# A ring of ten weight places split into six for gate/up and four for down, the down chunks issued by the scalar engine

## The chip, the cores and the metric
One core of a Trainium2 chip. The metric is the time of one execution on the device in microseconds; the median of three runs stands for a kernel.

## The reference
One decoder layer in fp32 for 288 tokens: 256 prompt tokens and 32 sample tokens (8 requests of 4) that read a paged cache. Three sub-layers, each followed by `LayerNorm(alpha * x + sublayer(x))`:

```python
mix  = merge_groups(moba(qa, ka, va), stick_breaking(qb, kb, vb), g_moba, g_sb, w_out)  # 16 heads of 64
x    = layer_norm(alpha * x + mix, ln1_g, ln1_b)
x    = layer_norm(alpha * x + mem_attend(x, mk, mv, w_mq, w_mo), ln2_g, ln2_b)           # 4 heads of 256, 256 memory tokens
...
logits = h @ w_router + b_router                      # 32 experts, the best 4 of each token
gate, up = split(h @ w_gu[e] + b_gu[e], 2)            # w_gu[e]: 1024 x 2048
act  = (clip(up, -7, 7) + 1) * min(gate, 7) * sigmoid(1.702 * min(gate, 7))
y    = act @ w_down[e] + b_down[e]                    # w_down[e]: 1024 x 1024
x    = layer_norm(alpha * x + sum of the 4 experts' y, weighted by their gates, ln3_g, ln3_b)
```

The weights of all 32 experts are read once: 8 MB of `w_gu` and 4 MB of `w_down` each, 403 million bytes in all.

## The kernel before
The program is written engine by engine with semaphores. Its first part (projections, both kinds of attention, the cross-attention) streams its inputs through six slots of 1 MB (`EARLY`, in the order of the list `ITEMS`) on the sync queue (SP). GpSimd (POOL) issues smaller loads and the stores of keys and values. Its first loads bring the rows of the norms' vectors into `vec_rows`, which TensorE turns into the columns of `vec` (wait on `vec_in` in line 662). Four of these loads (line 1288) bring the second norm's two vectors once more, every second element of each, for the pairs of columns that the gathered rows of the experts use (`by_seat`, line 2290).

The second part is the expert stage. An expert's weights come as six chunks of 2 MB: four of gate/up (256 rows of `w_gu` each) and two of down (512 rows of `w_down` each). There are ten places (`ALL`, `PLACES`, `chunk_slot`), and chunk `i`, counted over the experts in the order in which they run, takes place `i % 10`; so the place of a chunk was last held by the chunk ten before it. The sync engine issues all of them in this order (lines 1247 to 1259). Ahead of each it waits until the place is free (`slot_free`): `chunk_used` counts what TensorE has finished with, `gu_used` and `dn_used` stand for an expert's last gate/up and last down chunk, raised by VectorE and ScalarE. The first ten chunks are loaded while the first part ends, by `first_chunk`.

An expert runs in passes over at most 64 rows ("wide") or 32 ("narrow", two of four experts after the first group; `KINDS`), as many as its tokens need. All passes of an expert use the same chunks, and a place counts as free only in the last pass (`passes_done` in `enter`). The first four experts run in their own order, wide; the other 28 are sorted by the number of their tokens into an order of alternating wide and narrow ones (`order`, computed on the chip).

In a pass TensorE multiplies three gate/up chunks (line 1080), adds the output of the pass before (`combine`, lines 1014 and 1017), multiplies the fourth chunk, gathers the rows of the next pass (lines 1025 and 1033), turns the activations (1115) and multiplies the two down chunks (1125 in wide passes, 1129 in narrow ones). VectorE and ScalarE compute the activation in between; ScalarE's pass begins with the sigmoid (line 1815) and ends with the copy of the result out of bank 4, behind which it raises `dn_used`.

Of the kernel before, what the change touches and what calls it, by code (L numbers as in the profile page):

```python
# [68 lines left out]
HOME = 9760  # L69
PLACES = (8, 9, 6, 3, 0, 5, 7, 4, 1, 2)  # L70
EARLY = 6
# [84 lines left out]
def build(nc, A, O):  # L156
    ctx = ExitStack()
    with ctx:
        def sb(name, shape, dt=F32):
            return ctx.enter_context(nc.sbuf_tensor(name, shape, dt))  # L160

        def sem(name):
            return ctx.enter_context(nc.semaphore(name))
# [4 lines left out]
        pages = sb("pages", [1, NB_DEC * PAGES], I32)  # L168
        vec = sb("vec", [P, 56])
        small = sb("small", [P, 32])  # L170
# [17 lines left out]

        def chunk_slot(i):

            at = HOME + PLACES[i % ALL] * SLOT
# [33 lines left out]
        tmp = [at_place(6, 768 * i, 768) for i in range(5)] + [at_place(7, 768 * i, 768) for i in range(3)]  # L225
        vec_rows = at_place(6, 3840, P)[0:56]
        so = [at_place(7, 2304 + 512 * g, 512) for g in range(2)]
# [70 lines left out]
        gpick = [table("rot", P), table("new_strict", P), carve(mem, 6912, P)]  # L298
        ln3 = carve(mem, HOME + PLACES[NE * CHUNKS_E % ALL] * SLOT, 2, D)


        const_in = sem("const_in")
        pages_in = sem("pages_in")
        vec_in = sem("vec_in")
        early_in = [sem(f"early_in{i}") for i in range(EARLY)]
        item_used = sem("item_used")
        slot_in = [sem(f"slot_in{i}") for i in range(ALL)]
# [4 lines left out]
        dn_used = sem("dn_used")  # L312
        bank_full = [sem(f"bank_full{i}") for i in range(ROT)]
# [192 lines left out]
        def gu_src(e, k):  # L506
            return A["w_gu"][0, bass.ds(e, 1), 256 * k:256 * k + 256, :].rearrange("a (p r) n -> p (a r n)", p=P)
# [8 lines left out]
        def _(pe):  # L516
# [144 lines left out]
            pe.sem_inc(item_used, 4)  # L661
            pe.wait_ge(vec_in, 16 * 10)
            last, full = turn_blocks(("vec",), [vec_rows[:, :]])
# [379 lines left out]

            pe.sem_inc(chunk_used, CHUNKS_E - 2)
            pe.wait_ge(z_ready, 3)
# [11 lines left out]
            def chunk_arrived(group, q, j):  # L1057

                i = CHUNKS_E * (group * GROUP + q) + j
                pe.wait_ge(slot_in[i % ALL], 16 * (i // ALL + 1))  # L1060
                return chunk_slot(i)

# [6 lines left out]
            def expert_pass(group, q, kind):  # L1069
# [50 lines left out]
                for i in range(DN_CHUNKS):  # L1120
                    w = chunk_arrived(group, q, GU_CHUNKS + i).rearrange("p (r n) -> p r n", r=4)
                    for r in range(4):
                        for h in range(2):
                            if kind == CAP:
                                last = pe.matmul(bank[4][64 * h:64 * h + 64, :], actT[:, r, 64 * i:64 * i + 64],  # L1125
                                                 w[:, r, 512 * h:512 * h + 512], start=(i + r == 0), stop=(i == 1 and r == 3))
                            else:
                                at, t = 64 * h + 32 * (r % 2), 2 * i + r // 2
                                last = pe.matmul(bank[4][at:at + 32, :], actT[:, r % 2, 32 * t:32 * t + 32],  # L1129
                                                 w[:, r, 512 * h:512 * h + 512], start=(i == 0 and r < 2), stop=(i == 1 and r >= 2))  # L1130
                    if i == 0:
                        last.then_inc(chunk_used, 1)
                        turn_seats(n + 1)
# [23 lines left out]
        def _(sp):  # L1157
# [27 lines left out]

            def chunk(e, i):

                j = i % CHUNKS_E
                src = gu_src(e, j) if j < GU_CHUNKS else dn_src(e, j - GU_CHUNKS)
                sp.dma_start(chunk_slot(i), src).then_inc(slot_in[i % ALL], 16)  # L1190

            def first_chunk(i):
                chunk(i // CHUNKS_E, i)

# [39 lines left out]
            def slot_free(j, n):  # L1234

                if j == GU_CHUNKS - 1:
                    sp.wait_ge(gu_used, n)
                elif j == CHUNKS_E - 1:
                    sp.wait_ge(dn_used, n)
                else:  # L1240
                    sp.wait_ge(chunk_used, n * (CHUNKS_E - 2) + (j + 1 if j < GU_CHUNKS else j))

# [3 lines left out]

            for i in range(ALL, NE * CHUNKS_E + 1):
                if i == GROUP * CHUNKS_E:
                    sp.wait_ge(order_ready, 1)
                if i % CHUNKS_E == 0 or i == ALL:  # L1250
                    e = i // CHUNKS_E
                    if GROUP <= e < NE:
                        e = sp.value_load(order[0:1, e:e + 1], min_val=0, max_val=NE - 1)
                before, j = divmod(i - ALL, CHUNKS_E)
                if j == 0:
                    enter(before)
                slot_free(j, sp.snap(passes_done))
                if i < NE * CHUNKS_E:
                    chunk(e, i)
            for i, name in enumerate(("ln3_g", "ln3_b")):  # L1260
# [12 lines left out]
        def _(pool):  # L1273
# [211 lines left out]
        def _(act):  # L1485
# [122 lines left out]
            last.then_inc(read_sem(("vs",)), 1)  # L1608
            carry(("vec",), vec[:, :], wide(56))
            act.wait_ge(keys_stored, 16 * 2)  # L1610
# [200 lines left out]
            def expert_pass(kind):  # L1811
                n = act.snap(blocks_done)
                width = D * kind // P
                act.wait_ge(sig_in, n + 1)
                act.activation(sig_s[:, 0:width], gate_s[:, 0:width], ACT.Sigmoid, scale=SW_ALPHA).then_inc(sig_ready, 1)  # L1815
                act.wait_ge(sel_turned, n + 2)
                copy(selT, bank[5][:, 0:NPT])
                for h in range(2):
                    last = copy(sel_end[64 * h:64 * h + 64, h, :], bank[5][64 * h:64 * h + 64, NPT:T])
                last.then_inc(selT_ready, 1)  # L1820
                act.wait_ge(act_turned, n + 1)
                copy(actT[:, 0:width // P, :], bank[3][:, 0:width].rearrange("p (a b) -> p a b", b=P)).then_inc(actT_ready, 1)
                seats_in(n + 1)
                act.wait_ge(down_done, n + 1)
                act.sem_inc(dn_used, 1)
                copy(y_s, bank[4][:, :]).then_inc(y_ready, 1)
                act.reg_add(blocks_done, blocks_done, 1)

            def expert(e, kind):
                passes = act.value_load(passes_at[0:1, bass.ds(e, 1)], min_val=1, max_val=-(-T // kind))  # L1830
                with act.Fori(0, passes):
                    expert_pass(kind)

            for e in range(GROUP):
# [29 lines left out]
        def _(dve):  # L1864
# [424 lines left out]

            def by_seat(at):  # L2290
                return vec[:, at:at + KB].rearrange("p (h b) -> p b h", h=2).unsqueeze(3).broadcast_to([P, 4, 2, CAP])

            def seats_scale(n):

                dve.wait_ge(seats_turned, n + 1)
                x = xgT.rearrange("p (b h) s -> p b h s", h=2)
                dve.tensor_tensor(x, bank[0][:, :].rearrange("p (b h s) -> p b h s", b=4, h=2), by_seat(40), ALU.mult).then_inc(seats_scaled, 1)  # L2297
                dve.wait_ge(seats_scaled, n + 1)
                dve.tensor_tensor(x, x, by_seat(48), ALU.add).then_inc(xg_ready, 1)

# [178 lines left out]
```

## Time and profile before

| | |
|---|---|
| median of 3 runs | 1415.88 us (1411.34 to 1418.51) |
| the profiled execution | 1420.54 us, its span 1418.8 us |
| TensorE busy | 1303.4 us, 92% of the span |
| VectorE, ScalarE, GpSimd busy | 425.6, 238.1, 240.6 us |
| mean granted TensorE clock | 0.973 of full speed |
| read from HBM | 475.84 MB |
| copies, mean over the span | 340 GB/s |

The span runs from the first to the last instruction. A busy TensorE is not one at its peak. The DMA share is the mean busy share of the core's 16 copy engines in a stretch; it can read a little over 1. "SPq", "POOL" and "ACTq" with DMA_DIRECT2D are the instructions that issue a copy. An arrow in brackets names what ended the idle time before an instruction.

### The profile page before, as it was taken

Reading aid. Unit: us, or ns where it says so; the run is one execution under the profiler, and the core shown is the slowest. Engines: PE = TensorE matmul, PEld = TensorE weight load, DVE = VectorE, ACT = ScalarE, POOL = GpSimd, SP = SyncE. Lnnn points to the kernel's source line nnn. Section 1 sums busy time; section 2 is a strip of 40 time slices with the busy share of each in tenths; the row PEclk is TensorE's granted clock in tenths of the full one; section 3 lists DMA queues with packets and bytes.
Section 4 is the critical chain, followed back from the end, with each engine's and each line's share of the span. In section 5 each row is a group of like instructions: output and inputs, shape, how many; then the busy total and the mean of one; then the engine's idle time right before and its main releaser. Section 6 shows DMA issues by size and latency. Waiting matters only on the chain.

```text
span 1418.8 us, 22637 instructions
## 1 busy us (share of the span) xinstructions
PE 1303.4 (92%) x8246; PEld 637.7 (45%) x8246; DVE 425.6 (30%) x859; ACT 238.1 (17%) x537; POOL 240.6 (17%) x477
## 2 busy tenths in 40 slices
PE   6999688999889799999999999987999988899993
PEld 5787565677646333333333333322333333333331
DVE  1124544324432533223232132321131321222316
ACT  1124534211320201111110110100011100010102
POOL 4010001000101221212221122221121221122302
PEclk9999899999999799999999999999999999999997
DMA  9434429634489399999999999999999999999993
GB/s 253 142 123 151 150 84 333 204 119 148 181 327 418 143 399 428 431 430 430 428 430 432 431 429 431 430 429 431 430 423 429 431 431 428 431 432 415 429 430 137
DMA packets 73543, 482.74 MB, mean 340 GB/s; under 512 B 5146, under 2 KB 38098, under 8 KB 48658
## 3 DMA queue, kind: packets, MB, share of 16 engines
q1 hardware_dynamic: 71346, 475.29, 82.0%
q0 software_dynamic: 2064, 6.10, 1.3%
q8 instruction: 64, 1.05, 0.3%
q10 hardware_dynamic: 48, 0.13, 0.0%
q14 instruction: 21, 0.17, 0.0%
HBM read 475.84 MB, written 5.64 MB: 339 GB/s over the span
## 4 chain that ended last, share of the span: by engine, by line
PE 74%; DMA 18%; DVE 3%; issue 2%; ACT 2%; POOL 0%; SPq 0%; ACTq 0%; DVEq 0%; POOLq 0%; PEldq 0%
PE bank L1080 23%; DMA mem<-in_w_gu 13%; PE bank L547 10%; PE bank L1125 9%; PE bank L556 4%; PE bank L1025 4%; PE bank L1014 4%; DMA mem<-in_w_down 3%; PE bank L534 2%; PE bank L968 2%; PE bank L1129 2%; PE bank L1033 2%; DMA mem<-in_w_in 1%; PE bank L1115 1%; PE bank L1017 1%
## 5 line engine op out<-in xcount | busy, mean ns | idle before, releaser
L1080 PE MATMUL bank<-mem 128*32 128x256 f32 (+1 forms) x3136 | 419.6, 485 | 29.9 <-DMA mem<-in_w_gu 29.0
L1080 PEld LDWEIGHTS bank<-mem 128*32 128x32 f32 (+1 forms) x3136 | 152.2, 122 | 269.8 <-issue 200.2
L2360 DVE TENSOR_TENSOR mem<-mem,bank 128x512 f32<-128x512 f32 (+1 forms) x180 | 101.2, 627 | 431.9 <-PE bank L1014 431.9
L1497 ACT ACTIVATE mem<-bank 128x512 f32<-128x512 f32 (+7 forms) x236 | 114.2, 497 | 543.7 <-PE bank L1125 152.2
L547 PE MATMUL bank<-mem 128*128 128x288 f32 (+1 forms) x640 | 158.6, 405 | 7.1 <-PE bank L547 3.3
L1125 PE MATMUL bank<-mem 128*64 128x512 f32 x672 | 153.5, 598 | 0.0
L547 PEld LDWEIGHTS bank<-mem 128*128 128x128 f32 x640 | 121.4, 192 | 42.1 <-issue 8.4
L1438 POOL COPY mem<-mem 96x64 bf16 x35 | 11.5, 329 | 600.4 <-PE bank L1107 600.2
L1815 ACT ACTIVATE mem<-mem 128x512 f32<-128x512 f32 (+1 forms) x35 | 19.0, 544 | 491.3 <-DVE mem L2373 491.3
L2297 DVE TENSOR_TENSOR mem<-bank,vec 128x512 f32<-128x512 f32 x36 | 24.9, 691 | 201.8 <-PE bank L1041 201.8
L1878 DVE COPY mem<-bank 128x512 f32<-128x512 f32 (+3 forms) x82 | 47.5, 586 | 123.0 <-PE bank L534 37.7
L1125 PEld LDWEIGHTS bank<-mem 128*64 128x64 f32 x672 | 44.5, 136 | 84.0 <-issue 84.0
L534 PE MATMUL bank<-consts,mem 128*128 128x128 f32 (+3 forms) x449 | 58.7, 281 | 21.9 <-DMA mem<-in_x_prompt 7.3
L1025 PE MATMUL bank<-mem 128*64 128x512 f32 x288 | 74.4, 636 | 1.5 <-DVE mem L2263 1.5
L1014 PE MATMUL bank<-mem,consts 64*128 64x512 f32 x288 | 72.7, 623 | 1.0 <-ACT mem L1497 1.0
L556 PE MATMUL bank<-mem 128*128 128x256 f32 x256 | 62.5, 405 | 5.5 <-ACT mem L1497 5.5
L534 PEld LDWEIGHTS bank<-consts,mem 128*128 128x128 f32 (+3 forms) x449 | 50.1, 143 | 35.6 <-issue 29.3
L1434 POOL TENSOR_SCALAR mem<-mem 64x64 f32<-64x64 f32 (+1 forms) x140 | 64.7, 481 | 7.5 <-POOL mem L1428 7.5
L1447 POOL TENSOR_SCALAR consts<-mem 128x128 f32<-128x128 f32 x70 | 62.6, 899 | 7.5 <-POOL mem L1442 7.5
L556 PEld LDWEIGHTS bank<-mem 128*128 128x128 f32 x256 | 51.5, 204 | 15.7 <-issue 8.1
L1129 PE MATMUL bank<-mem 128*32 128x512 f32 x448 | 53.9, 598 | 1.7 <-DMA mem<-in_w_down 1.4
L1014 PEld LDWEIGHTS bank<-mem,consts 64*128 64x128 f32 x288 | 25.4, 190 | 43.2 <-issue 43.2
(246 smaller groups left out, 975.5 us busy)
## 6 DMA issues: line engine op xcount, KB each, us to landing
mem<-in_w_gu SPq DMA_DIRECT2D x128, 2048.0 KB, 25.5
mem<-in_w_down SPq DMA_DIRECT2D x64, 2048.0 KB, 26.6
mem<-in_w_in SPq DMA_DIRECT2D x12, 1024.0 KB, 9.9
mem<-in_w_mkv SPq DMA_DIRECT2D x8, 1024.0 KB, 9.3
mem<-in_cache_k SPq DMA_DIRECT2D x16, 512.0 KB, 7.2
mem<-in_cache_v SPq DMA_DIRECT2D x16, 512.0 KB, 5.8
mem<-in_cache_mem_k SPq DMA_DIRECT2D x8, 1024.0 KB, 4.8
mem<-in_cache_mem_v SPq DMA_DIRECT2D x8, 1024.0 KB, 5.6
```

The costliest lines, as they stand in the source:

```text
L534: last = pe.transpose(ps[0:cols, at:at + rows], src, C("ident", 0, rows, rows))
L547: last = pe.matmul(ps[:, 0:n], w[:, k, col:col + P], (mem_block(k) if src is None else src[:, k, 0:n]), start=(k == 0), stop=(k == KB - 1))
L556: last = pe.matmul(ps[0:r, 0:256], (mem_block(k) if src is None else src[:, k])[:, a:a + r], w[:, k, :], start=(k == 0), stop=(k == KB - 1))
L1014: pe.matmul(bank[COMB_BANK[2 * c + h]][:, :], selT[rows, P * c:P * c + P], y_s[rows, :], start=True, stop=True).then_inc(comb, 1)
L1025: pe.matmul(bank[0][64 * h:64 * h + 64, :], pick[:, c, :], z[:, c, :].rearrange("p (q h) -> p h q", h=2)[:, h], start=(c == 0), stop=False)
L1080: last = pe.matmul(to, ebias[0:96, 0:kind] if k is None else xgT[:, k, 0:kind], columns(src, j, t, kind), **flags)
L1125: last = pe.matmul(bank[4][64 * h:64 * h + 64, :], actT[:, r, 64 * i:64 * i + 64], w[:, r, 512 * h:512 * h + 512], start=(i + r == 0), sto ...
L1129: last = pe.matmul(bank[4][at:at + 32, :], actT[:, r % 2, 32 * t:32 * t + 32], w[:, r, 512 * h:512 * h + 512], start=(i == 0 and r < 2), s ...
L1434: pool.tensor_scalar(pick[0:r, c, :], slots_now[0:r, 0:CAP], rcol[0:r, c:c + 1], None, ALU.is_equal).then_inc(pool_step, 1)
L1447: pool.tensor_scalar(gpick[c], slots_now, rcol[:, c:c + 1], gcol[:, c:c + 1], ALU.is_equal, ALU.mult).then_inc(pool_step, 1)
L1497: return act.activation(out, in_, ACT.Copy, scale=scale)
L2360: dve.tensor_tensor(a, a, ps, ALU.add).then_inc(added, 1)
```

## The change
The ring of ten places is split: six for gate/up chunks (`GU_PLACES`) and four for down chunks (`DN_PLACES`), each with its own semaphores. The first ten loads are now the first expert's six, two gate/up chunks and both down chunks of the second. After that the sync engine issues gate/up chunks alone, each when the gate/up chunk six before it has been used. The down chunks of expert `e + 2` are issued by ScalarE (`next_down`) behind its last pass of expert `e`. `dn_used` is gone, and `chunk_used` counts three chunks a pass.

The four strided loads of the second norm's rows at the start are gone. In their place GpSimd issues two loads into a tile of its own, `pair_vec`, ahead of the loads of `b_gu`; VectorE waits for them once before the first expert.

```diff
-PLACES = (8, 9, 6, 3, 0, 5, 7, 4, 1, 2)
+GU_PLACES = (8, 9, 6, 3, 7, 4)
+DN_PLACES = (0, 5, 1, 2)
+GU_RING, DN_RING = len(GU_PLACES), len(DN_PLACES)
...
-        vec = sb("vec", [P, 56])
+        vec = sb("vec", [P, 40])
+        pair_vec = sb("pair_vec", [P, 2, 4, 2])
...
-            pe.wait_ge(vec_in, 16 * 10)
+            pe.wait_ge(vec_in, 16 * 6)
...
                     if i == 0:
-                        last.then_inc(chunk_used, 1)
                         turn_seats(n + 1)
...
             def first_chunk(i):
-                chunk(i // CHUNKS_E, i)
+                if i < 4:
+                    gate_up(0, i)
+                elif i in (6, 7):
+                    gate_up(1, i - 2)
+                else:
+                    d = {4: 0, 5: 1, 8: 2, 9: 3}[i]
+                    down(d // DN_CHUNKS, d)
...
                 if j == GU_CHUNKS - 1:
                     sp.wait_ge(gu_used, n)
-                elif j == CHUNKS_E - 1:
-                    sp.wait_ge(dn_used, n)
                 else:
-                    sp.wait_ge(chunk_used, n * (CHUNKS_E - 2) + (j + 1 if j < GU_CHUNKS else j))
+                    sp.wait_ge(chunk_used, n * (GU_CHUNKS - 1) + j + 1)
...
-            for i in range(ALL, NE * CHUNKS_E + 1):
+            for g in range(GU_RING, NE * GU_CHUNKS + 1):
...
-                before, j = divmod(i - ALL, CHUNKS_E)
+                before, j = divmod(g - GU_RING, GU_CHUNKS)
...
-            for name, at in (("ln2_g", 40), ("ln2_b", 48)):
-                for h in range(2):
-                    pool.dma_start(vec_rows[at + 4 * h:at + 4 * h + 4, :], A[name][0].rearrange("(a p h) -> h a p", p=P, h=2)[h],
-                                   allow_slow_non_contiguous=True).then_inc(vec_in, 16)
...
             await_fill(pool, ("o", PAIR_ORDER[-2]))
+            for i, name in enumerate(("ln2_g", "ln2_b")):
+                pool.dma_start(pair_vec[:, i], A[name][0].rearrange("(b p h) -> p b h", p=P, h=2), allow_slow_non_contiguous=True).then_inc(pair_vec_in, 16)
             for part in range(3):
                 pool.dma_start(bgu_f[32 * part:32 * part + 32, :], A["b_gu"][0]).then_inc(bias_in, 16)
...
                 act.wait_ge(down_done, n + 1)
-                act.sem_inc(dn_used, 1)
                 copy(y_s, bank[4][:, :]).then_inc(y_ready, 1)
...
+            def next_down(e, i):
+
+                for d in range(DN_CHUNKS):
+                    at = DN_CHUNKS * i + d
+                    act.dma_start(dn_place(at), dn_src(e, d)).then_inc(dn_in[at % DN_RING], 16)
...
             for e in range(GROUP):
                 expert(e, FIRST[e])
+                if e + 2 < GROUP:
+                    next_down(e + 2, e % 2)
+                else:
+                    if e + 2 == GROUP:
+                        act.wait_ge(order_ready, 1)
+                    next_down(act.value_load(order[0:1, e + 2:e + 3], min_val=0, max_val=NE - 1), e % 2)
-            act.wait_ge(order_ready, 1)
-            with act.Fori(GROUP // 2, NE // 2) as pair:
+            with act.Fori(GROUP // 2, NE // 2 - 1) as pair:
                 for i in range(2):
                     expert(pair * 2 + i, KINDS[i])
+                    next_down(expert_at(pair * 2 + i + 2), i)
+            for i in range(2):
+                expert(NE - 2 + i, KINDS[i])
...
+            dve.wait_ge(pair_vec_in, 16 * 2)
```

## Rows read from the trace of the kernel before

**Rows 1.** The page: one engine's total, and GB/s in 40 slices.
```profile
PE 1303.4 (92%) x8246; PEld 637.7 (45%) x8246; DVE 425.6 (30%) x859; ACT 238.1 (17%) x537; POOL 240.6 (17%) x477
...
GB/s 253 142 123 151 150 84 333 204 119 148 181 327 418 143 399 428 431 430 430 428 430 432 431 429 431 430 429 431 430 423 429 431 431 428 431 432 415 429 430 137
```

**Rows 2.** Stretches: from:to, length, engines' busy time (count), clock, DMA share, GB/s.
```profile
510.00:520.00 10.00, 10.00 (x54) 3.76 (x54) 1.38 (x2) 1.79 (x3) 4.23 (x9) 1.00 0.92 360
...
494.00:1392.00 898.00, 867.91 (x5893) 320.06 (x5889) 233.18 (x393) 100.98 (x244) 186.96 (x374) 0.99 1.00 427
200.00:240.00 40.00, 32.62 (x272) 21.42 (x273) 15.07 (x34) 14.64 (x28) 3.68 (x9) 0.91 0.72 248
```

**Rows 3.** Timeline of TensorE: start, length, what; a wide, a narrow, a double expert.
```profile
605.39 7.04 PE L1080 MATMUL bank<-mem 128*64 128x512 f32 x32
...
634.28 3.83 PE L1080 MATMUL bank<-mem 128*32 128x256 f32 x64
...
642.48 2.02 PE L1080 MATMUL bank<-mem 128*32 128x256 f32 x32
...
652.70 2.79 PE L1080 MATMUL bank<-mem 128*64 128x512 f32 x12
...
750.25 8.78 PE L1080 MATMUL bank<-mem 128*64 128x512 f32 x32 [2.76 <-DMA mem<-in_w_gu]
...
765.93 3.65 PE L1080 MATMUL bank<-mem 128*64 128x512 f32 x16
...
781.39 7.04 PE L1080 MATMUL bank<-mem 128*64 128x512 f32 x32
```

**Rows 4.** The page's groups of instructions: the down products of wide passes.
```profile
L1125 PE MATMUL bank<-mem 128*64 128x512 f32 x672 | 153.5, 598 | 0.0
```

**Rows 5.** Waits: who, for whom: us in total, times, longest.
```profile
PE bank L882 <- DMA mem<-in_cache_mem_v: 2.9, 1, 2.9
...
ACT mem L1815 <- DVE mem L2373: 491.3, 35, 21.4
```

**Rows 6.** Stretches of the start, columns as in rows 2.
```profile
9.00:21.00 12.00, 10.63 (x50) 8.15 (x48) 1.41 (x4) 1.76 (x4) 7.31 (x5) 1.00 1.19 129
25.00:40.00 15.00, 14.70 (x54) 11.04 (x55) 2.75 (x6) 1.06 (x3) 0.00 (x0) 0.90 1.09 384
```

**Rows 7.** Timeline of TensorE at the start.
```profile
24.73 5.72 PE L547 MATMUL bank<-mem 128*128 128x288 f32 x16 [2.90 <-DMA mem<-in_w_in]
...
30.77 4.04 PE L547 MATMUL bank<-mem 128*128 128x288 f32 x16
```

**Rows 8.** Timeline of the sync queue and of ScalarE in the expert stage.
```profile
493.89 0.33 SPq L1190 DMA_DIRECT2D mem<-in_w_down  x1
...
515.07 0.33 SPq L1190 DMA_DIRECT2D mem<-in_w_gu  x1
...
519.35 0.60 ACT L1497 ACTIVATE mem<-bank 128x512 f32<-128x512 f32 x1 [7.26 <-PE bank L1125]
...
785.18 0.33 SPq L1190 DMA_DIRECT2D mem<-in_w_down  x1
...
810.57 0.33 SPq L1190 DMA_DIRECT2D mem<-in_w_gu  x1
```

**Rows 9.** One line's copies, from 485 to 560 us: issue to landing.
```profile
DMA to landing us min/median/max: 7.7/11.2/14.3
```

**Rows 10.** DMA issues: queue, count, KB each, median us to landing.
```profile
mem<-in_w_mo SPq DMA_DIRECT2D x4, 1024.0 KB, 14.0
...
out_new_k_prompt<-mem POOLq DMA_DIRECT2D x1, 1024.0 KB, 4.6
...
out_mem_v_prompt<-mem POOLq DMA_DIRECT2D x1, 1024.0 KB, 7.7
out_mem_k_prompt<-mem POOLq DMA_DIRECT2D x1, 1024.0 KB, 9.3
```

**Rows 11.** Timeline of TensorE: the last down products.
```profile
1393.32 1.92 PE L1129 MATMUL bank<-mem 128*32 128x512 f32 x16 [0.57 <-DMA mem<-in_w_down]
```

More of the change, by code:

```diff
@@ L187, in carve, with gu_place, dn_place @@
             return v
-        def chunk_slot(i):
-            at = HOME + PLACES[i % ALL] * SLOT
+        def gu_place(g):
+            at = HOME + GU_PLACES[g % GU_RING] * SLOT
+            return mem[:, at:at + SLOT]
+        def dn_place(d):
+            at = HOME + DN_PLACES[d % DN_RING] * SLOT
             return mem[:, at:at + SLOT]
@@ L225, in build @@
         tmp = [at_place(6, 768 * i, 768) for i in range(5)] + [at_place(7, 768 * i, 768) for i in range(3)]
-        vec_rows = at_place(6, 3840, P)[0:56]
+        vec_rows = at_place(6, 3840, P)[0:40]
         so = [at_place(7, 2304 + 512 * g, 512) for g in range(2)]
@@ L298, in build @@
         gpick = [table("rot", P), table("new_strict", P), carve(mem, 6912, P)]
-        ln3 = carve(mem, HOME + PLACES[NE * CHUNKS_E % ALL] * SLOT, 2, D)
+        ln3 = gu_place(NE * GU_CHUNKS)[:, 0:2 * D].rearrange("p (a n) -> p a n", a=2)
         const_in = sem("const_in")
@@ L304, in build @@
         vec_in = sem("vec_in")
+        pair_vec_in = sem("pair_vec_in")
         early_in = [sem(f"early_in{i}") for i in range(EARLY)]
         item_used = sem("item_used")
-        slot_in = [sem(f"slot_in{i}") for i in range(ALL)]
+        gu_in = [sem(f"gu_in{i}") for i in range(GU_RING)]
+        dn_in = [sem(f"dn_in{i}") for i in range(DN_RING)]
         bias_split = sem("bias_split")
@@ L311, in build @@
         gu_used = sem("gu_used")
-        dn_used = sem("dn_used")
         bank_full = [sem(f"bank_full{i}") for i in range(ROT)]
@@ L1042, in turn_seats @@
                 last.then_inc(seats_turned, 1)
-            pe.sem_inc(chunk_used, CHUNKS_E - 2)
+            pe.sem_inc(chunk_used, GU_CHUNKS - 1)
             pe.wait_ge(z_ready, 3)
@@ L1057, in chunk_arrived @@
             def chunk_arrived(group, q, j):
-                i = CHUNKS_E * (group * GROUP + q) + j
-                pe.wait_ge(slot_in[i % ALL], 16 * (i // ALL + 1))
-                return chunk_slot(i)
+                e = group * GROUP + q
+                if j < GU_CHUNKS:
+                    g = GU_CHUNKS * e + j
+                    pe.wait_ge(gu_in[g % GU_RING], 16 * (g // GU_RING + 1))
+                    return gu_place(g)
+                d = DN_CHUNKS * e + j - GU_CHUNKS
+                pe.wait_ge(dn_in[d % DN_RING], 16 * (d // DN_RING + 1))
+                return dn_place(d)
             def columns(v, j, t, kind):
@@ L1184, in early, with gate_up, down @@
                     sp.dma_start(dst, src[0, item[1]].rearrange("(c p) h d -> p c (h d)", p=P)).then_inc(s, 16)
[L1186 to L1190, printed above, removed]
+            def gate_up(e, g):
+                sp.dma_start(gu_place(g), gu_src(e, g % GU_CHUNKS)).then_inc(gu_in[g % GU_RING], 16)
+            def down(e, d):
+                sp.dma_start(dn_place(d), dn_src(e, d % DN_CHUNKS)).then_inc(dn_in[d % DN_RING], 16)
             def first_chunk(i):
-                chunk(i // CHUNKS_E, i)
+                if i < 4:
[5 more added lines that the diff above has]
+                    down(d // DN_CHUNKS, d)
             for i, item in enumerate(ITEMS):
@@ L1237, in slot_free @@
                     sp.wait_ge(gu_used, n)
-                elif j == CHUNKS_E - 1:
-                    sp.wait_ge(dn_used, n)
                 else:
-                    sp.wait_ge(chunk_used, n * (CHUNKS_E - 2) + (j + 1 if j < GU_CHUNKS else j))
+                    sp.wait_ge(chunk_used, n * (GU_CHUNKS - 1) + j + 1)
             def enter(at):
                 sp.reg_add(passes_done, passes_done, sp.value_load(passes_at[0:1, at:at + 1], min_val=1, max_val=PASS_MAX))
-            for i in range(ALL, NE * CHUNKS_E + 1):
-                if i == GROUP * CHUNKS_E:
+            for g in range(GU_RING, NE * GU_CHUNKS + 1):
+                if g == GROUP * GU_CHUNKS:
                     sp.wait_ge(order_ready, 1)
-                if i % CHUNKS_E == 0 or i == ALL:
-                    e = i // CHUNKS_E
+                if g % GU_CHUNKS == 0 or g == GU_RING:
+                    e = g // GU_CHUNKS
                     if GROUP <= e < NE:
                         e = sp.value_load(order[0:1, e:e + 1], min_val=0, max_val=NE - 1)
-                before, j = divmod(i - ALL, CHUNKS_E)
+                before, j = divmod(g - GU_RING, GU_CHUNKS)
                 if j == 0:
@@ L1257, in _ @@
                 slot_free(j, sp.snap(passes_done))
-                if i < NE * CHUNKS_E:
-                    chunk(e, i)
+                if g < NE * GU_CHUNKS:
+                    gate_up(e, g)
             for i, name in enumerate(("ln3_g", "ln3_b")):
@@ L1608, in _ @@
             last.then_inc(read_sem(("vs",)), 1)
-            carry(("vec",), vec[:, :], wide(56))
+            carry(("vec",), vec[:, :], wide(40))
             act.wait_ge(keys_stored, 16 * 2)
@@ L1832, in expert, with expert_at @@
                     expert_pass(kind)
+            def next_down(e, i):
+                for d in range(DN_CHUNKS):
+                    at = DN_CHUNKS * i + d
+                    act.dma_start(dn_place(at), dn_src(e, d)).then_inc(dn_in[at % DN_RING], 16)
+            def expert_at(at):
+                return act.value_load(order[0:1, bass.ds(at, 1)], min_val=0, max_val=NE - 1)
             for e in range(GROUP):
                 expert(e, FIRST[e])
-            act.wait_ge(order_ready, 1)
-            with act.Fori(GROUP // 2, NE // 2) as pair:
+                if e + 2 < GROUP:
[5 more added lines that the diff above has]
+            with act.Fori(GROUP // 2, NE // 2 - 1) as pair:
                 for i in range(2):
                     expert(pair * 2 + i, KINDS[i])
+                    next_down(expert_at(pair * 2 + i + 2), i)
+            for i in range(2):
+                expert(NE - 2 + i, KINDS[i])
             load_table(ACT.Sqrt)
@@ L2288, in _, with by_seat @@
             dve.tensor_tensor(gates, expo, small[:, 8:11].unsqueeze(2).broadcast_to([P, 3, NE]), ALU.mult).then_inc(gates_ready, 1)
-            def by_seat(at):
-                return vec[:, at:at + KB].rearrange("p (h b) -> p b h", h=2).unsqueeze(3).broadcast_to([P, 4, 2, CAP])
+            def by_seat(i):
+                return pair_vec[:, i].unsqueeze(3).broadcast_to([P, 4, 2, CAP])
+            dve.wait_ge(pair_vec_in, 16 * 2)
             def seats_scale(n):
@@ L2296, in seats_scale @@
                 x = xgT.rearrange("p (b h) s -> p b h s", h=2)
-                dve.tensor_tensor(x, bank[0][:, :].rearrange("p (b h s) -> p b h s", b=4, h=2), by_seat(40), ALU.mult).then_inc(seats_scaled, 1)
+                dve.tensor_tensor(x, bank[0][:, :].rearrange("p (b h s) -> p b h s", b=4, h=2), by_seat(0), ALU.mult).then_inc(seats_scaled, 1)
                 dve.wait_ge(seats_scaled, n + 1)
-                dve.tensor_tensor(x, x, by_seat(48), ALU.add).then_inc(xg_ready, 1)
+                dve.tensor_tensor(x, x, by_seat(1), ALU.add).then_inc(xg_ready, 1)
             seats_scale(0)
```

## The prediction
> **What bounds the kernel now.** I began with the page's totals [rows 1]: TensorE is busy 92% of the span, and from about a third of the span on some 430 GB/s arrive. Two engines near their limit are not decided by shares, so I took the stretches next [rows 2]. From 494 to 1392 us the DMA share is 1.00 and 427 GB/s arrive. A chunk of 2048 KB is 2.097 MB, so at 427 GB/s it costs 4.91 us, an expert of six chunks 29.5 us.
>
> What TensorE would need is read from its own rows [rows 3]: a wide pass lasts from 605.39 to 634.28, 28.9 us, a narrow one from 634.28 to 652.70, 18.4 us. The number of passes follows from the wide down products: 672 at 32 a pass are 21 passes [rows 4], and of 35 passes in all [rows 5] 14 are left as narrow. There are 18 wide experts (four first, then fourteen of 28), so 3 passes are second passes: three wide experts run twice. 21 x 28.9 + 14 x 18.4 = 865 us, against 898 us that the bytes take. The copies set the end, by 33 us, and TensorE's 92% includes no more slack than that. So each microsecond in which the copy engines stand idle after 494 us is added to the time, and work of TensorE is worth something only behind the last chunk.
>
> **The start (gain).** Removed are four loads of strided single elements (2048 elements of 4 bytes). From 9 to 21 us the DMA share is 1.19 and yet only 129 GB/s arrive, against 384 from 25 to 40 us [rows 6]: 12 x (1 - 129/384) = 8.0 us of copying lost. TensorE feels 2.90 us of it, where it waits for the second block of `w_in`, and the granted clock falls after that wait: the next 16 products took 5.72 us where the following 16 took 4.04, 1.68 us more [rows 7]. Sum 2.90 + 1.68 = 4.6 us, if the block comes 2.9 us earlier, for which 8.0 is enough. Bounds: 0, and 8.0 if all of the copying counted; I take 4.6. Afterwards TensorE waits for a copy only once before the experts, 2.9 us at L882 [rows 5], behind loads that its own progress releases; so the gain travels on.
>
> The two new loads (1024 pieces of 8 bytes) stand in the GpSimd queue ahead of the `b_gu` loads at about 212 us. At the price above for a piece, 8.0/2048 us, they are 4.0 us of copying. Between 200 and 240 us the DMA share is 0.72 [rows 2] and no wait of TensorE's there is for a copy, so I take 0 and keep 4.0 as the other bound. VectorE's new wait for them comes some 270 us later. The `b_gu` loads behind them move by the two issues; VectorE takes them up only behind the first layer norm.
>
> **ScalarE as issuer.** It takes over 60 of the 64 down issues at 0.33 us as on the sync queue, about 1 us an expert with the register loads. Behind them on its queue waits the sigmoid, for which ScalarE idles 491 us over 35 passes, 14 us each [rows 5]. Cost 0; without that cover it would be 1 us an expert, 32 us. No later step waits for these instructions, since the copy of the result precedes them. The narrower vector table (40 rows for 56) is one small copy: nothing.
>
> **The places.** This is the main term. Both kernels have ten places. Before, any chunk takes the next one, in the order of need. After, an expert's four gate/up chunks use six places and its two down chunks four, and a down chunk is asked for only when the expert two before it has ended (last pass), where before each place was refilled as it came free.
>
> First expert. Its four gate/up chunks release copies from 493.89 on [rows 8] in both kernels; back to back they last to about 493.9 + 4 x 4.91 = 513.5 (plus the lead). Before, the next issue is at 515.07, released by the first down chunk: a hole of 1.5, which the slice from 510 confirms (360 GB/s for 427: 1.6 us) [rows 2]. After, that place goes to the down ring, and the next issue is ScalarE's, behind its copy of 519.35 + 0.60: 520.0. Hole 6.5. Difference 5.0 us.
>
> The three experts with two passes. During the first pass nothing of the expert is released. From the start of the last gate/up chunk to the second pass is 781.39 - 765.93 = 15.5 us, the first chunk of the second pass 3.5 (half of 7.04) [rows 3]: 19.0 us until a place comes free. A lone chunk lands 7.7 us after its issue [rows 9], so 2.8 us are lead and tail. For 19.0 + 2.8 = 21.8 us the copy engines live on what was outstanding when that last chunk landed, 4.91 us a chunk. Four places are not held by the expert: two of gate/up, two of down. The first pass begins with TensorE waiting for gate/up (2.76 us at 750.25) [rows 3], and the two down chunks of the next expert were issued before it. If the two queues share the engines equally, these two land while two gate/up chunks do, so before the fourth: two chunks are left, 9.8 us, and the hole is 12.0 us. (Before, the copies came in order of need, so the expert's own two down chunks and four of the next were still to come, 29.5 us, and the hole is closed.)
>
> Then the second pass releases four gate/up chunks one after the other: copies for 19.6 us from 785.18. Before, the two down places follow, the last at 810.57 [rows 8], and the stream never dries. After, the next are ScalarE's at the end of the pass, 810.57 + 0.6 + 0.3, 26.3 us after the first: a second hole, 26.3 - 19.6 = 6.7. Together 18.7 us an expert, three times 56.1 us.
>
> What is late next is the gate/up stream as a whole; TensorE waits there, but that is inside the same microseconds and is not counted again.
>
> Share of the second queue. No row shows two hardware queues at once. Nearest is GpSimd's queue beside the sync queue: the same 1024 KB store landed in 4.6 us with little beside it, in 7.7 us amid value loads and in 9.3 us amid weights [rows 10]. It got ahead of weights queued earlier (those took 14 us for as many bytes), so not by arrival; something between a third and a half. I take a half, for packets of equal size, and keep arrival order as the bound.
>
> The Trainium skill (DMA: Bandwidth & Descriptors, Queues, rings and completion order) says that a copy engine goes round its queues packet by packet; by that the half holds and the sum would be as below. It agrees with the store's rows as far as they go.
>
> The end. Before, the last chunk is the second down chunk of the last expert; TensorE starts it at 1393.32 and 1.9 us later all products are done [rows 11]. After, down chunks are asked for two experts ahead and the last to land is a gate/up chunk; a narrow expert then still has 652.70 - 642.48 = 10.2 us to go [rows 3]. 8.3 us more. Rest of the tail unchanged.
>
> **Sum.** -4.6 + 5.0 + 56.1 + 8.3 = +64.8 us on the profiled execution's 1420.5 (span 1418.8 and 1.7 around it): 1485.3. That execution lies 4.7 above the median of 1415.9, from which it would be 1480.7. I say 1483.
>
> **Rivals.** (a) Down chunks come in order of arrival or with a smaller share. Then the next expert's two are still outstanding, four chunks are left, and the first hole is 21.8 - 19.6 = 2.2: 5.0 + 3 x (2.2 + 6.7) + 8.3 - 4.6 = +35.4, about 1454; with a third of the bandwidth, in step with use, somewhat less, 1445. For it: the 9.3 us. Against: the 7.7 us.
>
> (b) Not slower: two queues together carry more than one. The mechanism sits in the stream from 494 to 1392: to make up 64.8 us of 898, 427 GB/s would have to become 460; from there on it is a gain, to a floor of 1420.5 - 33 - 4.6 = 1383 where TensorE alone bounds. For it: the rate does depend on the transfers' form (384 with the early weights, 427 here). Against: a share of 1.00 leaves no free engine time to fill.
>
> The Trainium skill (DMA: Bandwidth & Descriptors, Rules for kernel authors) says that spreading loads over issuing engines does not raise bandwidth, as they run on the same engines; by that (b) falls.
>
> (c) The holes don't arise because TensorE is far enough behind when the double passes come, and only start and end count: 1420.5 - 4.6 + 8.3 = 1424. Against: ten places less the six held leave four chunks, 19.6 us, for 21.8.
>
> (d) Worse: the waits before double passes lower the granted clock, as after the wait at 24.73, and lengthen the holes, by some 2 us in 18.7 or more: above 1500.
>
> **Numbers.** Chances: forecast 0.60 (own range 1465 to 1500), (a) 0.24, (b) 0.07, (c) 0.04, (d) 0.05. The range has to hold forecast and (a), which give 1440 to 1500. A measurement of this kernel tells about 0.5%, 7 us, from no change. Faster is (b), 0.06; the rest of it and (c), 0.05, no change; slower 0.89.
>
> **What would show it.** In the stretches: holes in the DMA share of about 6 us at 514 and of 12 and 7 us at three places in the expert stage, 1.00 between them, and the same 430 GB/s there. TensorE waits for gate/up and hardly for down. The last chunk to land is gate/up. The first stall at 24.73 is gone and the experts begin about 4.6 us earlier. Wrong would be: no holes at the double passes (sharing or the count of chunks left), a rate above 440 in full slices, or holes at ordinary experts, which would make it longer.

## The result and the profile after

The changed kernel takes 1492.8 us (median of 4 runs, 1491.0 to 1496.5) against 1417.2 us (4 runs of the kernel before, 1411.3 to 1420.4): ratio 1.053 [1.050, 1.055], slower. The forecast was 1483 us. Its profiled execution took 1492.8 us, with a span of 1491.1; against the span of before (1418.8) that is 72.3 us, and the sum below is made on it.

First the page of the kernel after: TensorE's total, the 40 slices of the DMA share and of GB/s, and the two hardware queues that now carry weights (packets, MB, share).

```profile
PE 1329.4 (89%) x8246; PEld 640.5 (43%) x8246; DVE 425.9 (29%) x859; ACT 238.1 (16%) x537; POOL 237.4 (16%) x475
...
DMA  8326159435596699999996899999689999959990
GB/s 289 113 89 229 57 171 341 135 114 226 188 408 268 251 428 427 428 430 430 431 430 269 359 429 431 430 429 431 271 353 431 430 429 430 418 226 410 430 425 37
...
q1 hardware_dynamic: 62706, 349.45, 57.7%
q10 hardware_dynamic: 8688, 125.96, 20.1%
```

TensorE has the same 8246 matmuls as in [rows 1], and the rate in undisturbed slices is the same 430 GB/s. New are three pairs of low slices in the expert stage (269 and 359, 271 and 353, 226 and 410), one for each expert with two passes. Finer stretches put bounds on them (columns as in [rows 2]):

```profile
510.00:520.00 10.00, 10.00 (x48) 3.38 (x48) 1.38 (x2) 1.15 (x2) 2.31 (x7) 1.00 0.50 188
...
790.00:800.00 10.00, 10.00 (x53) 3.88 (x53) 3.34 (x5) 1.85 (x5) 5.44 (x11) 1.00 0.39 169
800.00:810.00 10.00, 10.00 (x52) 3.47 (x50) 0.12 (x1) 0.60 (x1) 0.00 (x0) 1.00 0.29 86
...
820.00:830.00 10.00, 10.00 (x52) 3.71 (x50) 2.72 (x4) 1.48 (x5) 5.20 (x10) 1.00 0.74 318
830.00:840.00 10.00, 10.00 (x142) 4.88 (x142) 1.98 (x4) 0.60 (x1) 0.00 (x0) 1.00 0.72 270
```

One minus the share, times the length, is the time in which the copy engines stood idle. At the first expert it is 5.0 us, where before had 0.8. At the first double expert it is 6.1 + 7.1 = 13.2 us and then 2.6 + 2.8 = 5.4. The other two have the same pair: 13.1 and 5.9 from 1040 to 1090, and 13.0 and 5.9 from 1300 to 1350. In all of these stretches but one TensorE is busy for 10.00 us of 10 (9.82 from 1040 to 1050): it isn't waiting there, it is working through chunks that hold their places.

The timeline of TensorE (start, length, what, and in brackets the wait before and for whom) at the start, at the first double expert and at the end:

```profile
13.01 9.58 PE L556 MATMUL bank<-mem 128*128 128x288 f32 x32 [0.83 <-DVE mem L1911]
...
23.45 4.04 PE L556 MATMUL bank<-mem 128*128 128x288 f32 x16
...
27.82 4.04 PE L556 MATMUL bank<-mem 128*128 128x288 f32 x16
...
150.16 6.65 PE L565 MATMUL bank<-mem 128*128 128x256 f32 x16 [4.12 <-ACT mem L1514]
157.54 3.72 PE L565 MATMUL bank<-mem 128*128 128x256 f32 x16
...
486.73 9.02 PE L1094 MATMUL bank<-mem 128*64 128x512 f32 x32 [0.99 <-DVE mem L2334]
...
786.61 3.65 PE L1094 MATMUL bank<-mem 128*64 128x512 f32 x16 [1.64 <-DMA mem<-in_w_gu]
...
802.08 7.04 PE L1094 MATMUL bank<-mem 128*64 128x512 f32 x32
...
1425.69 5.35 PE L1094 MATMUL bank<-mem 128*64 128x512 f32 x16 [4.13 <-DMA mem<-in_w_gu]
...
1457.36 2.02 PE L1094 MATMUL bank<-mem 128*32 128x256 f32 x32
...
1465.72 1.92 PE L1143 MATMUL bank<-mem 128*32 128x512 f32 x16
```

And the two issuers in the same double expert, the sync queue's first gate/up copy of the second pass and ScalarE's two down copies behind its copy of the result:

```profile
806.20 0.34 SPq L1201 DMA_DIRECT2D mem<-in_w_gu  x1
...
831.08 0.60 ACT L1514 ACTIVATE mem<-bank 128x512 f32<-128x512 f32 x1 [7.16 <-PE bank L1139]
831.97 1.42 ACTq L1854 DMA_DIRECT2D mem<-in_w_down  x2
```

The first hole is read from these: the last gate/up chunk arrives at 786.61 and no place comes free until 806.20, 19.6 us. The second as well: four chunks released from 806.20 last 19.6 us, to about 825.8 and a lead; the next copies are asked for at 831.97.

That the two queues share is seen between 747 and 757 us, where both always have work: the two down chunks asked for at 744.1 and 744.6 land 14.6 and 23.8 us later, the three gate/up chunks asked for from 745.32 on after 31.6 to 42.3 us. (The columns are packets, MB and share of the 16 engines; then come the landing times of both over the whole run, with count, KB each and median us.)

```profile
DMA packets 286, 4.33 MB, mean 433 GB/s; under 512 B 22, under 2 KB 22, under 8 KB 22
...
q1 hardware_dynamic: 151, 2.21, 51.6%
q10 hardware_dynamic: 134, 2.10, 49.2%
...
mem<-in_w_gu SPq DMA_DIRECT2D x128, 2048.0 KB, 31.7
...
mem<-in_w_down ACTq DMA_DIRECT2D x60, 2048.0 KB, 17.3
```

Half each, and together hardly more than the 430 GB/s that one queue had carried. The Trainium skill (DMA: Bandwidth & Descriptors, Queues, rings and completion order) says that an engine goes round its queues by packets; this trace agrees, with 51.6 and 49.2% (51.0 and 50.1 from 758 to 767 us). So a down chunk that is needed a whole expert later takes half of the rate from the gate/up chunk that is needed next.

### The profile page after: what moved, and what is told of

It is laid out like the page before. It is cut to its first block, busy times and chain, and to the rows that moved or that the text cites. A ratio compares the mean times of both kernels' runs of the same rounds, so it can differ in the third digit from the quotient of the medians.

```text
span 1491.1 us, 22649 instructions
## 1 busy us (share of the span) xinstructions
PE 1329.4 (89%) x8246; PEld 640.5 (43%) x8246; DVE 425.9 (29%) x859; ACT 238.1 (16%) x537; POOL 237.4 (16%) x475
## 4 chain that ended last, share of the span: by engine, by line
PE 67%; DMA 25%; DVE 3%; issue 2%; ACT 2%; POOL 0%; SPq 0%; ACTq 0%; DVEq 0%; POOLq 0%; PEldq 0%
DMA mem<-in_w_gu 24%; PE bank L1094 19%; PE bank L556 11%; PE bank L1139 10%; PE bank L565 4%; PE bank L1034 4%; PE bank L543 3%; PE bank L1023 2%; PE bank L977 2%; PE bank L1042 2%; PE bank L1143 1%; PE bank L1129 1%; PE bank L1050 1%; PE bank L870 1%; PE bank L1121 1%
## 5 line engine op out<-in xcount | busy, mean ns | idle before, releaser
L1094 PE MATMUL bank<-mem 128*32 128x256 f32 (+1 forms) x3136 | 445.8, 502 | 79.3 <-DMA mem<-in_w_gu 78.3
L1094 PEld LDWEIGHTS bank<-mem 128*32 128x32 f32 (+1 forms) x3136 | 155.7, 126 | 342.7 <-issue 196.7
L2332 DVE TENSOR_TENSOR mem<-bank,pair_vec 128x512 f32<-128x512 f32 x36 | 24.9, 691 | 202.2 <-PE bank L1050 202.2
L543 PEld LDWEIGHTS bank<-consts,mem 128*128 128x128 f32 (+3 forms) x449 | 50.1, 144 | 35.4 <-issue 29.1
```

Of the source, the lines that this page charges most:

```text
L543: last = pe.transpose(ps[0:cols, at:at + rows], src, C("ident", 0, rows, rows))
L1094: last = pe.matmul(to, ebias[0:96, 0:kind] if k is None else xgT[:, k, 0:kind], columns(src, j, t, kind), **flags)
```

## The experiments

The theory was: places that an expert holds over its passes, together with down chunks asked for early on a queue that takes half, make the copy engines run dry; each idle microsecond is added to the time. Its rivals were: the second queue or ScalarE as issuer costs something by itself; and TensorE is the bound. Each time is a median, with a ratio to runs of the kernel before on the same chip (1418.9 us over 23 runs for the first four, 1418.8 over 7 for the last two).

**The moved rows alone.** The kernel before, with nothing of the change but the second norm's rows loaded later.

```diff
-            for name, at in (("ln2_g", 40), ("ln2_b", 48)):
-                for h in range(2):
-                    pool.dma_start(vec_rows[at + 4 * h:at + 4 * h + 4, :], A[name][0].rearrange("(a p h) -> h a p", p=P, h=2)[h],
...
+            for i, name in enumerate(("ln2_g", "ln2_b")):
+                pool.dma_start(pair_vec[:, i], A[name][0].rearrange("(b p h) -> p b h", p=P, h=2), allow_slow_non_contiguous=True).then_inc(pair_vec_in, 16)
```

> The kernel before with only the moved loads of the second norm's rows; ring and queues as before. If the start is worth what the changed kernel's profile shows at its first expert (488.30 against 486.73 us), 1.6 us faster than before, 1415.6; TensorE's stall of 2.9 us at 24.73 gone, the first expert's products at about 486.7. The rival, that the prediction's 4.6 us are there and the ring hides them, gives 1412.6 and the first products at 483.7. Copies at 1.00 from there on in both.

Measured: 1416.6 us (12 runs, 1407.0 to 1418.4), ratio 0.997 [0.995, 0.999]. That is a gain, of 4.3 us by the ratio (between 1.3 and 7.2) and of 2.2 by the two medians. Both 1.6 and 4.6 us lie in the interval, and the times don't decide between them. The stretch of [rows 6] and the timeline of TensorE show what happens:

```profile
9.00:21.00 12.00, 10.52 (x48) 8.05 (x48) 1.57 (x3) 1.83 (x4) 2.92 (x3) 1.00 1.07 391
```

```profile
21.28 4.04 PE L549 MATMUL bank<-mem 128*128 128x288 f32 x16
...
25.64 4.04 PE L549 MATMUL bank<-mem 128*128 128x288 f32 x16
...
147.89 5.25 PE L558 MATMUL bank<-mem 128*128 128x256 f32 x16 [4.12 <-ACT mem L1497]
153.87 3.72 PE L558 MATMUL bank<-mem 128*128 128x256 f32 x16
...
481.70 8.98 PE L1082 MATMUL bank<-mem 128*64 128x512 f32 x32 [0.99 <-DVE mem L2301]
```

Some 391 GB/s arrive where 129 did, the third block starts at 25.64 instead of 30.77, and the experts begin at 481.70 instead of 488.30: in this execution the start is worth 6.6 us. Of the kernels that ran on this chip it is the fastest.

**Second passes left out, in the kernel before.** Three passes, and the rows that need them, are missing from the output.

```diff
-            step(dve.tensor_scalar(passes_both, passes_both, 1.0, None, ALU.add))
+            step(dve.tensor_scalar(passes_both, passes_both, 0.0, 1.0, ALU.mult, ALU.add))
```

> The kernel before with every expert run for one pass: the second passes of the three large experts are left out, so some tokens get no result from them. The copies set the end in both readings, so the time stays at that of before, 1417 within 3 us, though TensorE has 3 x 28.9 = 87 us less to do.

Measured: 1418.5 us, ratio 1.000 [0.998, 1.001]. Three passes of 28.9 us each, 87 us of TensorE's work, are gone and the time doesn't move. The copies set the end of the kernel before; TensorE as the bound falls.

**Second passes left out, in the kernel after.** The same edit.

> The changed kernel with every expert run for one pass (the second passes are left out as in the run beside it). If the loss comes from the places that a second pass holds, the holes of 13 and 5.5 us at three places vanish with it (56 us) and only start, first hole and tail are left: -1.6 + 5 + 13, some 16 us above before, 1433, with one hole of 5 us at about 514. If the loss comes from the second hardware queue or from ScalarE as issuer (60 copies, whatever the passes), it stays near 60 us above before, 1475 or more, and the stretches of the expert stage run below 1.00 or below 425 GB/s throughout.

Measured: 1429.2 us (4 runs), ratio 1.008 [1.005, 1.011], which is 7 to 16 us more than the kernel before. With the same rings, the same second queue and the same issuer, 64 of the 76 us that the change costs are gone. Some 57 of them are the holes at the double experts, and 7 an earlier start (the experts begin at 479.33 in this profile, at 486.73 in that of the changed kernel). The stretches:

```profile
500.00:510.00 10.00, 10.00 (x52) 3.85 (x52) 1.59 (x3) 1.28 (x3) 4.52 (x9) 1.00 0.59 250
510.00:520.00 10.00, 10.00 (x50) 3.39 (x48) 0.00 (x0) 0.51 (x1) 0.00 (x0) 1.00 0.91 351
...
494.00:1386.00 892.00, 793.05 (x5295) 286.05 (x5291) 200.50 (x341) 89.76 (x217) 168.82 (x335) 0.95 1.00 426
```

Only the hole at the first expert is left (4.1 + 0.9 us); from there on the share is 1.00 at 426 GB/s, on two queues and with ScalarE issuing. So neither costs anything by itself. In this run TensorE still waits 99.0 us for gate/up: such waits were no loss here, where the copies never stopped.

What is left besides is the end. These stretches show it (the columns as before):

```profile
1380.00:1390.00 10.00, 10.00 (x124) 4.53 (x120) 0.89 (x2) 0.60 (x1) 0.00 (x0) 1.00 0.47 197
1390.00:1400.00 10.00, 10.00 (x95) 4.02 (x97) 4.76 (x11) 2.05 (x6) 0.00 (x0) 1.00 0.01 2
1400.00:1410.00 10.00, 3.46 (x28) 0.93 (x16) 7.32 (x15) 3.91 (x6) 1.29 (x1) 0.87 0.00 0
```

The copies end at about 1384.7, and TensorE's last down products end at 1400.90, 16 us later; before, 3 us lay between (below).

**One queue, places as in the change, down asked for at the expert's end.** The rings of six and four places stay; all copies go out on the sync queue. An expert's down chunks stand behind the copy that the last gate/up chunk of the expert two before releases, and are issued when that expert has ended (`dn_used`, here raised behind ScalarE's copy of the result).

```diff
                 gate_up(e, g)
+                if j == GU_CHUNKS - 1:
+                    sp.wait_ge(dn_used, sp.snap(passes_done))
+                    for d in range(DN_CHUNKS):
+                        down(e, DN_CHUNKS * (before + 2) + d)
...
-            def next_down(e, i):
...
-                    act.dma_start(dn_place(at), dn_src(e, d)).then_inc(dn_in[at % DN_RING], 16)
```

> The changed kernel with its two rings, but the down chunks issued by the sync queue, in the order in which their places come free, still at the end of the expert two before. All copies are one queue again. If equal sharing brings the down chunks in ahead of need, that is undone: four chunks instead of two are outstanding when a large expert's last gate/up chunk lands, the first hole shrinks from 13 to about 2.5 us, the second stays at 6 to 7, and the time falls by about 30 us to 1459, still 42 above before. If the second queue is the whole cause, the time is that of before, 1416. If the queue doesn't matter and only the release at the expert's end does, it stays at 1490.

Measured: 1463.1 us (4 runs), ratio 1.032 [1.029, 1.035].

```profile
510.00:520.00 10.00, 10.00 (x52) 3.42 (x50) 0.00 (x0) 0.60 (x1) 0.00 (x0) 1.00 0.76 283
...
780.00:790.00 10.00, 10.00 (x54) 3.84 (x52) 1.76 (x3) 1.19 (x2) 4.70 (x9) 1.00 0.77 331
790.00:800.00 10.00, 10.00 (x52) 3.40 (x50) 0.00 (x0) 0.60 (x1) 0.00 (x0) 1.00 0.57 202
...
810.00:820.00 10.00, 10.00 (x69) 3.72 (x72) 1.38 (x2) 1.79 (x3) 3.48 (x8) 1.00 0.51 213
```

The first holes shrink from 13.1 to 6.6, 7.1 and 5.6 us, which is less than expected (2.5; the rows of the next experiment show why). The second ones stay near 5 (4.9, 4.7, 4.9). The time falls by 30 us, 1492.8 - 1463.1, as expected, but not all of that is the order of the copies. By the profiles (spans 1491.1 and 1459.6) 22.7 us are the smaller holes at the double experts, 56.5 less 33.8. Another 5.6 us are an earlier start of the experts (481.13 for 486.73) and 4.3 a shorter end (9.5 us from the end of the copies to the last product). Queue and issuer were changed together here; that half of the rate goes to the down chunks is read from the shares above. What stays, 33.8 us of holes and the longer end, is there with one queue too.

**The same, and each down place asked for again as it comes free.** A semaphore raised after the first down chunk lets the sync queue issue one at a time, and the other is raised ahead of the copy of the result (as in the kernel before, whose code raises `dn_used` ahead of that copy and not behind it).

```diff
-                    sp.wait_ge(dn_used, sp.snap(passes_done))
-                    for d in range(DN_CHUNKS):
+                    for d, used in enumerate((dn0_used, dn_used)):
+                        sp.wait_ge(used, sp.snap(passes_done))
                         down(e, DN_CHUNKS * (before + 2) + d)
...
+                        last.then_inc(dn0_used, 1)
```

> The changed kernel's two rings with all copies on the sync queue, and each down place refilled as soon as its own chunk has been used in the last pass, not at the expert's end. Against the run with one queue and release at the end (1463) this takes away the late release alone. If the late release makes the second hole of a large expert and the hole at 514, these shrink from 6 to 7 us to 1.5 each and the time falls by 20 to 22 us to 1441; left are a first hole of some 2.5 us at three places and the longer end. If the division into rings is what costs, whatever the release, it stays at 1460.

Measured: 1452.3 us (4 runs), ratio 1.024 [1.020, 1.028]: some 11 us less than the experiment above, about half of what was expected. The holes that the late release made were smaller than the 6 to 7 us counted on, 19.2 us in all with the one at 514 (4.7), and fall to 4.0; the start and the end are 1.0 and 1.5 us longer. The stretches of the first double expert, and two rows of TensorE in it:

```profile
760.00:770.00 10.00, 6.91 (x20) 2.15 (x22) 0.00 (x0) 0.00 (x0) 0.00 (x0) 0.66 1.00 428
...
780.00:790.00 10.00, 10.00 (x50) 3.48 (x48) 1.39 (x2) 0.94 (x2) 2.10 (x7) 1.00 0.48 206
790.00:800.00 10.00, 10.00 (x50) 3.22 (x45) 0.65 (x2) 0.00 (x0) 0.00 (x0) 1.00 0.81 311
...
810.00:820.00 10.00, 10.00 (x102) 4.17 (x102) 1.38 (x2) 0.60 (x1) 2.10 (x6) 1.00 0.91 339
```

```profile
763.09 6.30 PE L1096 MATMUL bank<-mem 128*64 128x512 f32 x16 [5.46 <-DMA mem<-in_w_gu]
...
771.82 3.65 PE L1096 MATMUL bank<-mem 128*64 128x512 f32 x16
```

The second holes are nearly closed, as expected (4.9 to 0.9 us). The first ones stay at 5.2 + 1.9 = 7.1, 6.9 and 5.9 us, where 2.5 was expected, and the reason is seen in the rows. The last gate/up chunk isn't waited for at 771.82; the last wait is for the third, 5.46 us, and its 16 products took 6.30 us at a granted clock of 0.66, instead of 3.6. From 763.09 to the first release at about 790.8 are 27.7 us, with lead and tail 30.5. Five chunks were outstanding, 24.6 us: 6 us are missing, 2.7 of them by the lowered clock. At the other two double experts the same products took 6.58 and 5.06 us, 2.9 and 1.4 more than at full clock, and the smallest hole is where they lost least. The experiment above has the same rows (5.97, 6.60 and 5.17 us).

**The kernel before with the double experts early.** Any chunk takes any place again, and one queue carries all; only the order of the experts changes, so that the double ones come while TensorE doesn't yet wait for copies: chunks land ahead of their need, and few are outstanding.

```diff
-    places = wide[3::4] + wide[2::4] + wide[1::4] + wide[0::4] + narrow[0::2] + narrow[1::2][::-1]
+    places = wide + narrow[0::2] + narrow[1::2][::-1]
```

> The kernel before with its ring of ten and one queue; only the order of the experts differs: the wide ones run by falling number of tokens, so that the three with two passes are the 5th, 7th and 9th expert instead of the 11th, 19th and 27th. If the holes come from places that a second pass holds while too little is outstanding, they appear in the old ring too where TensorE has not yet fallen behind the copies: holes of about 24, 15 and 15 us between 600 and 800 us, and a time some 60 us above before, 1478. If they come from the split into two rings or two queues, this order costs nothing and the time stays at 1418.

Measured: 1480.0 us (4 runs), ratio 1.043 [1.039, 1.048].

```profile
610.00:620.00 10.00, 10.00 (x54) 3.28 (x52) 3.38 (x6) 0.00 (x0) 0.00 (x0) 1.00 0.43 182
620.00:630.00 10.00, 10.00 (x53) 3.77 (x51) 2.66 (x5) 2.47 (x6) 5.43 (x11) 1.00 0.01 2
630.00:640.00 10.00, 10.00 (x51) 3.31 (x49) 0.92 (x2) 0.60 (x1) 0.00 (x0) 1.00 0.24 70
```

A hole of 5.7 + 9.9 + 7.6 = 23.2 us at the first of them, 14.1 and 14.2 at the other two, on ten common places and one queue. From 494 to 800 us no wait of TensorE's is for a copy. The five chunks asked for from 580 to 606 us, just ahead of the first double expert, landed in 13.8 us (median). In the kernel before the six asked for from 730 to 766, around the start of its first double expert, took 43.9: so much more was still outstanding ahead of them. The split isn't needed for a hole: what makes it is an expert that keeps its places for two passes while too little else is outstanding. The split of the change, with down chunks that arrive too early, is one way to have too little outstanding; the order of experts is another.

## Why the prediction was right

The direction, the mechanism and the main term held; the start and the end were mis-sized, by 3.0 and 2.4 us, both towards a time that was too low. Against the span of before, in the profiled execution:

| term | predicted | measured | from |
|---|---|---|---|
| start | -4.6 | -1.6 | first expert's products begin at 486.73, before at 488.30 |
| first expert's hole | +5.0 | +4.2 | share 0.50 for 0.92 |
| three double experts | +56.1 | +56.5 | 18.6 + 19.0 + 18.9 |
| end | +8.3 | +10.7 | end of the copies to the last product: 13.8 for 3.1 |
| not assigned | | +2.5 | 0.3% of the stage |
| sum | +64.8 | +72.3 | spans |

**Double experts.** The formula for the first hole (21.8 us less 4.91 for each chunk outstanding) gave 12.0, and the time between two releases gave 6.7 for the second; measured were 13.1 and 5.7 on average. That the sum agrees to 0.4 us is partly luck: one error is 1.1 too low, the other 1.0 too high. The prediction's 19.0 us from the last gate/up chunk to the first release are 19.6 in the rows above, and with two chunks left 19.6 + 2.8 - 9.8 = 12.6. The half share on which the two chunks rest is now shown directly (51.6 and 49.2%), and the experiment fits it: with one queue the first hole is about half. So (a), arrival order or a smaller share, falls. (b), two queues that carry more, falls with 433 GB/s where both are full (428 to 432 in full slices of the kernel before). (c), no holes, falls by the stretches.

**The lowered clock, (d).** It is there: behind waits of 4.13 and 5.46 us the products of a chunk took 5.35 and 6.30 us, for 3.6. In the kernel after it doesn't lengthen the holes at the double experts, since the last wait there is short (1.64 us, at the other two 0.18 and 0.38), the products behind it take 3.65 us and the clock is 1.00 in 790 to 810. In the one-queue kernel that refills by chunk it does, by 2.7, 2.9 and 1.4 us.

**The end.** The step that was mis-sized is "the last to land is a gate/up chunk; a narrow expert then still has ... 10.2 us to go". The first half holds: the last weights to land are gate/up (asked for at 1421.30, landed 31.9 us later, the last down chunk asked for at 1408.3). The 10.2 us were counted from the chunk's arrival, as if TensorE stood waiting for it. But TensorE was late: its last long wait for gate/up ends at 1425.69, from there it has 42 us of work of its own to 1467.64, and it takes the last chunk only at 1457.36. By the share of these stretches the copies end about 1453.8, 13.8 us before the last product:

```profile
1440.00:1450.00 10.00, 10.00 (x64) 3.79 (x66) 1.38 (x2) 1.79 (x3) 1.78 (x3) 1.00 1.02 436
1450.00:1460.00 10.00, 10.00 (x149) 5.07 (x139) 3.57 (x7) 0.47 (x2) 0.00 (x0) 1.00 0.38 157
```

In the kernel before the same reading gives 1392.1, and 3.1 us to the end of [rows 11]:

```profile
1390.00:1400.00 10.00, 7.23 (x56) 2.19 (x52) 3.92 (x6) 2.68 (x4) 0.00 (x0) 1.00 0.21 86
```

The run without second passes repeats it: 16 us.

**The start.** The stall of [rows 7] is gone, as predicted, and the third block begins 2.95 us earlier, at 27.82 (in the moved-rows kernel 5.13 earlier). That the gain "travels on" holds for the moved rows, and did not in this execution of the kernel after: the first 32 products took 9.58 us where the other has 8.00, and at 150.16 the 16 products behind the wait for ScalarE took 6.65 us where the other has 5.25. Together that makes 3.0 of the 5.0 us that lie between 486.73 and 481.70. The stretches of the kernel after around both:

```profile
12.00:23.00 11.00, 9.87 (x35) 7.22 (x35) 0.88 (x2) 0.79 (x2) 0.04 (x1) 1.00 1.08 383
...
150.00:160.00 10.00, 9.84 (x35) 7.70 (x36) 1.82 (x5) 2.26 (x10) 0.00 (x0) 0.69 0.00 0
```

The second goes with a lowered granted clock (0.69, with the moved rows alone 0.95). The first doesn't as far as the profile shows: the clock reads 1.00 there in both kernels. The late start needn't come from the change. The three other kernels that were profiled with its rings and its moved rows began their experts at 479.33 (second passes left out), 481.13 and 482.09 us (one queue); and the kernel before with the double experts early, which has nothing of the change, also took 9.59 us for the first 32 products. But the other executions of the kernel after took 1491.0 to 1496.5 us, and none of them is 5 us faster than the profiled one. These runs don't settle why. The loads moved to 212 us cost nothing, as forecast: no wait of TensorE's there is for a copy.

## What to carry to other kernels

Where copies set the end, count for each moment how many are outstanding while the slowest consumer holds its places: chunks left times the time of one, against the time to the next release. A pool that any chunk may enter in the order of need covered such a stretch where TensorE was waiting for copies (1417 us), and not where chunks landed ahead of need (1480 us); fixed shares of the same places, refilled at the end of a step, covered less of it, and a second queue that runs ahead used up the cover by carrying what is needed last. And look at small strided loads that stand beside the first weights: moving 2048 elements away from them was the one part of this change that paid, with 0.3% of the time.

## What the runs showed of the hardware

Two hardware queues shared the copy engines 51.6 to 49.2% over 10 us (264 of the 286 packets there of some 16 KB, the others under 512 B), and the sum (433 GB/s) was close to that of one queue (430). The order of need was lost by that: with one queue the holes at the double experts were 22.7 us smaller.

A wait of TensorE for data can cost more than its length. In the kernel after, the 16 products behind a wait of 4.13 us took 5.35 us, and in the one-queue kernel 6.30 us behind 5.46, at a granted clock of 0.66 over 760 to 770 us (a mean over its two levels, 1.2 and 2.4 GHz), for 3.65 us at full clock. Not each wait did so: at 1277.61 us of the kernel after the same products took 3.65 us behind a wait of 3.70. Where it happens ahead of a second pass, it lengthens the time for which places are held, and so comes back as idle copy engines.
